# Expert output parts stacked on 128 partitions, gathered rows as half rows on 128 partitions, and the last output tile by weight rows

## The reference, cut to what matters

```python
def hier_moe(x, w_group, w_expert, w_gate, w_up, w_down):
    ...
    weight = g_w * e_w / jnp.sum(e_w, -1, keepdims=True)
    expert = (g_idx * M_PER_GROUP + e_idx).reshape(-1)
    token = jnp.repeat(jnp.arange(n_tok), M_TOPK)
    order = jnp.argsort(expert)
    tok_sorted = token[order]
    sizes = jnp.bincount(expert, length=M_EXPERTS).astype(jnp.int32)
    xs = xt[tok_sorted]
    hid = jax.nn.silu(lax.ragged_dot(xs, w_gate, sizes)) * lax.ragged_dot(xs, w_up, sizes)
    ys = lax.ragged_dot(hid, w_down, sizes) * weight.reshape(-1)[order][:, None].astype(x.dtype)
    return jax.ops.segment_sum(ys, tok_sorted, num_segments=n_tok).reshape(b, s, d)
```

## Time and profile before

| what | us |
|---|---|
| median of 3 runs | 2735.05 |
| range of the runs | 2734.01 to 2735.18 |
| time of the profiled execution | 2735.55 |
| its span, first to last instruction | 2733.7 |
| PE busy | 2618.6 (96%) |
| DVE busy | 1461.6 (53%) |
| ACT busy | 749.7 (27%) |

### The profile page before, as it was taken

One profiled execution on the slowest core, in us unless ns is written; L12 is line 12 of the kernel. 1 busy time (PEld: TensorE's weight loads), 2 busy tenths in 40 slices (PEclk: granted clock), 3 DMA queues, 4 the chain that ended last, 5 costly groups with the idle time before them and its releaser, 6 DMA issues. The chain is left out here.

```text
span 2733.7 us, 39425 instructions
## 1 busy us (share of the span) xinstructions
PE 2618.6 (96%) x15526; PEld 1859.7 (68%) x15526; DVE 1461.6 (53%) x2028; ACT 749.7 (27%) x1205; POOL 114.4 (4%) x238
## 2 busy tenths in 40 slices
PE   8997999999799979999999699999999999999999
PEld 7674555555476665555555577888888877888887
DVE  4755444444654554444444676656552666556632
ACT  3530000000145510000000343543332454433331
POOL 0000000000000000000000000000000010000000
PEclk9998999999899989999999899999999999999999
DMA  6249999999322089999997132223332312223331
GB/s 171 82 169 373 388 409 408 411 407 401 116 77 93 37 309 388 405 405 403 408 405 299 53 106 77 93 77 102 99 123 93 101 62 93 78 93 99 102 123 54
DMA packets 168109, 559.82 MB, mean 205 GB/s; under 512 B 17394, under 2 KB 100914, under 8 KB 118322
## 3 DMA queue, kind: packets, MB, share of 16 engines
q1 hardware_dynamic: 162546, 549.68, 53.4%
q0 software_dynamic: 5440, 8.40, 1.0%
HBM read 561.17 MB, written 6.29 MB: 208 GB/s over the span
## 5 line engine op out<-in xcount | busy, mean ns | idle before, releaser
L1401 DVE TENSOR_TENSOR resid<-resid,ps 128x1024 f32<-128x1024 f32 x252 | 306.8, 1218 | 237.7 <-PE ps L1321 237.7
L229 PE MATMUL ps<-l_h_hi,l_w_hi 128*128 128x512 f32 x896 | 352.9, 394 | 0.0
L230 PE MATMUL ps<-l_h_lo,l_w_hi 128*128 128x512 f32 x896 | 348.8, 389 | 0.0
L231 PE MATMUL ps<-l_h_hi,l_w_lo 128*128 128x512 f32 x896 | 348.7, 389 | 0.0
L1308 PE MATMUL ps<-first_weights,moe_xsT 128*64 128x256 f32 x2688 | 326.2, 384 | 0.0
L2885 DVE TENSOR_TENSOR l_w_lo<-l_raw,l_w_hi 128x2048 fp32r<-128x2048 f32 x76 | 174.0, 2292 | 270.6 <-ACT l_w_hi L2630 270.3
L1308 PEld LDWEIGHTS ps<-first_weights,moe_xsT 128*64 128x64 f32 x2688 | 191.5, 137 | 133.0 <-issue 67.4
L1373 ACT ACTIVATE moe_ys_hi<-ps 128x512 fp32r<-128x512 f32 x64 | 38.2, 597 | 687.3 <-PE ps L1347 687.3
L2630 ACT ACTIVATE l_w_hi<-l_raw 128x2048 fp32r<-128x2048 f32 x76 | 145.6, 1918 | 180.6 <-PE ps L231 161.1
L229 PEld LDWEIGHTS ps<-l_h_hi,l_w_hi 128*128 128x128 f32 x896 | 168.2, 188 | 37.6 <-issue 2.9
L230 PEld LDWEIGHTS ps<-l_h_lo,l_w_hi 128*128 128x128 f32 x896 | 168.3, 188 | 35.4 <-issue 1.4
(11 more groups left out here) (611 smaller groups left out, 4621.8 us busy)
## 6 DMA issues: line engine op xcount, KB each, us to landing
first_weights<-in_moe_w_up SPq DMA_DIRECT2D x84, 1024.0 KB, 11.5
first_weights<-in_moe_w_down SPq DMA_DIRECT2D x84, 1024.0 KB, 10.4
first_weights<-in_moe_w_gate SPq DMA_DIRECT2D x84, 1024.0 KB, 11.2
first_ring<-in_moe_w_up SPq DMA_DIRECT2D x44, 1024.0 KB, 11.7
first_ring<-in_moe_w_down SPq DMA_DIRECT2D x44, 1024.0 KB, 10.7
l_raw<-in_ffn_up SPq DMA_DIRECT2D x44, 1024.0 KB, 5.1
first_ring<-in_moe_w_gate SPq DMA_DIRECT2D x40, 1024.0 KB, 10.9
l_raw<-in_w_in SPq DMA_DIRECT2D x22, 1024.0 KB, 5.2
```

Of the source, the lines that this page charges most:

```text
L229: pe.matmul(out, stationary[0], moving[0], start=first, stop=False)
L230: pe.matmul(out, stationary[0], moving[1], start=False, stop=False)
L231: return pe.matmul(out, stationary[1], moving[0], start=False, stop=last)
L1401: dve.tensor_tensor(row, row, sums(t), ALU.add).then_inc(added, 1)
```

## The change

1. **Stacked parts.** One tile `ys` of 128 partitions x 2 x 512 takes the place of `ys_hi` and `ys_lo`. For column half 0 the high part stands on partitions 0-63 and the low part on 64-127, for half 1 the other way round. A combine is now two products of 128 rows. ACT makes the high part in two copies of 64 partitions, DVE the low part in two subtractions of 64 partitions; a subtraction writes the partitions that it doesn't read. Both count up one semaphore, `parts_made` (with `sel`, three to a block), on which the next combine waits.
2. **Half rows.** `xs` is 128 partitions x 512: slot s takes columns 0-511 of its row on partition s and columns 512-1023 on partition 64 + s. The gathers read 128 half rows of 2 KB instead of 64 rows of 4 KB, `r.take` is twice the row's number plus the half, and `lay` makes it for 128 partitions at once, after both halves of PE's list. The 8 transposes now alternate between partitions 0-63 (into bank 0) and 64-127 (into bank 1). The gate sums move to bank 1 and the up sums and turned hidden values to bank 3.
3. **Waits on PE.** The waits on `hid_kept` at a block's start and on `ys_low` ahead of the down product go; one on `silued` ahead of the turn of the rows comes.
4. **The last token tile of the output products** goes by weight rows: both column halves over the first four blocks of weight rows, then both over the last four. After the first four SP may start pieces of expert 0 (four of the six: up and down in the first layer, gate and up in the second), the other two after the last product. The third `keep_rows` stands ahead of that wait on SP.

The diff, cut to its core:

```diff
@@ Routing.lay @@
         dve.wait_ge(x.listed, 1)
-        dve.tensor_copy(x.near[0:SLOTS, :], k.ps[0:SLOTS, 3, 0:COLS]).then_inc(x.near_kept, 1)
-        dve.wait_ge(x.near_kept, 1)
-        dve.scalar_tensor_tensor(r.take[0:SLOTS, :], k.ps[0:SLOTS, 3, COLS:2 * COLS], float(NO_ROW), x.near[0:SLOTS, :], ALU.add, ALU.add).then_inc(x.done, 1)
+        link(dve.tensor_scalar(x.near[:, :], k.ps[:, 3, 0:COLS], float(NO_ROW), None, ALU.add))
+        link(dve.tensor_tensor(r.token, k.ps[:, 3, COLS:2 * COLS], x.near[:, :], ALU.add))
+        dve.tensor_scalar(r.take[:, :], r.token, 2.0, k.cst[:, C_HALF:C_HALF + 1], ALU.mult, ALU.add).then_inc(x.done, 1)
...
@@ window_layer, sync @@
             keep_rows(2)
+            sp.wait_ge(upper_used, 1)
+            weights.load(sp, layer, 0, 0, lambda c: None, range(2, 6))
             sp.wait_ge(am.out_made, 2 * NT)
-            weights.load(sp, layer, 0, 0, lambda c: None, range(6))
+            weights.load(sp, layer, 0, 0, lambda c: None, range(2))
...
@@ window_layer, out_part @@
-                half = q // 2
+                half, quarter = (q // 2, q % 2) if t + 1 < NT else (q % 2, q // 2)
...
@@ experts, tensor @@
             def turn_rows():
-                for j in range(ND):
-                    ins = pe.transpose(k.ps[:, TURN, j * SLOTS:(j + 1) * SLOTS], row_of_tile[:, j // 4, j % 4, :], k.cst[0:SLOTS, C_ID:C_ID + SLOTS])
+                for i in range(4):
+                    for c in range(2):
+                        rows_ = slice(64 * c, 64 * c + 64)
+                        ins = pe.transpose(turned[:, c, i * SLOTS:(i + 1) * SLOTS], row_of_tile[rows_, i, :], k.cst[rows_, C_ID + 64 * c:C_ID + 64 * c + 64])
...
                 if t == 0:
-                    wait_then_tick(pe, sel_made, b + 2, tick_pe)
-                    wait_then_tick(pe, ys_low, b + 2, tick_pe)
+                    wait_then_tick(pe, parts_made, 3 * b + 4, tick_pe)
...
-                for part in (ys_hi, ys_lo):
-                    for h in range(2):
-                        rows_ = slice(64 * h, 64 * h + 64)
-                        ins = pe.matmul(sums(t)[:, h, :], sel[rows_, t * P:(t + 1) * P], part[rows_, :], start=part is ys_hi, stop=part is ys_lo)
+                for h in range(2):
+                    ins = pe.matmul(sums(t)[:, h, :], sel[:, t * P:(t + 1) * P], ys[:, h, :], start=True, stop=True)
...
-                wait_then_tick(pe, ys_low, b + 1, tick_pe)
...
@@ experts, scalar @@
-                act.activation(ys_hi[:, :], k.ps[:, DOWN, :], ACT.Copy).then_inc(ys_kept, 1)
+                for h in range(2):
+                    rows_ = slice(64 * h, 64 * h + 64)
+                    act.activation(ys[rows_, h, :], k.ps[rows_, DOWN, :], ACT.Copy).then_inc(ys_kept, 1)
@@ experts, vector @@
-                dve.wait_ge(ys_kept, b + 1)
-                dve.tensor_tensor(ys_lo[:, :], k.ps[:, DOWN, :], ys_hi[:, :].bitcast(F32), ALU.subtract).then_inc(ys_low, 1)
+                for h in range(2):
+                    high, low = slice(64 * h, 64 * h + 64), slice(64 - 64 * h, P - 64 * h)
+                    dve.wait_ge(ys_kept, 2 * b + h + 1)
+                    dve.tensor_tensor(ys[low, h, :], k.ps[high, DOWN, :], ys[high, h, :].bitcast(F32), ALU.subtract).then_inc(parts_made, 1)
```

More of the change, by code:

```diff
@@ L426, in lay @@
         ins.then_inc(x.laid, 1)
[L427 to L430 removed]
+        dve.wait_ge(x.listed, 2)
         link(dve.tensor_copy(x.near[:, :], k.ps[:, 7, 0:COLS]))
@@ L762, in out_part @@
             def out_part(t, q):
-                half = q // 2
+                half, quarter = (q // 2, q % 2) if t + 1 < NT else (q % 2, q // 2)
                 if q == 0:
                     pe.wait_ge(o_lo, WIN_DONE[t])
-                if q % 2 == 0 and 0 < 2 * t + half < 5:
+                if quarter == 0 and 0 < 2 * t + half < 5:
                     pe.wait_ge(am.evacuated, 2 * t + half)
-                if (t, q) == (3, 2):
+                if (t, q) == (3, 1):
                     pe.wait_ge(am.evacuated, 5)
-                for j in range(4 * (q % 2), 4 * (q % 2) + 4):
+                for j in range(4 * quarter, 4 * quarter + 4):
                     if t == 0 and half == 0 and j % 2 == 0:
@@ L775, in out_part @@
                                        [y[:, j % 2, half * 512:(half + 1) * 512] for y in (hi, lo)], j == 0, j == ND - 1)
-                if q % 2:
+                if quarter:
                     ins.then_inc(am.out_made, 1)
+                elif (t, half) == (3, 1):
+                    ins.then_inc(upper_used, 1)
             pe.wait_ge(ident_in, 16)
@@ L1205, in experts @@
     silu, hid, hidT = st.sb("silu", [P, 256]), st.sb("hid", [P, 256]), st.sb("hidT", [P, 2, P])
-    take, slot = st.sb("take", [SLOTS, 1], I32), st.sb("slot", [P, 2, 1])
-    ys_hi, ys_lo, sel, iota = st.sb("ys_hi", [P, 512], F32R), rt.ys_lo, rt.sel, rt.iota
-    (take_set, slot_set, rows_turned, xsT_kept, silued, hid_kept, hid_turned, hidT_kept, ys_kept, ys_low, sel_made, combined, added, tick_sp, tick_pool, tick_pe, chain,
+    take, slot = st.sb("take", [P, 1], I32), st.sb("slot", [P, 2, 1])
+    ys, sel, iota = rt.ys, rt.sel, rt.iota
+    (take_set, slot_set, rows_turned, xsT_kept, silued, hid_kept, hid_turned, hidT_kept, ys_kept, parts_made, combined, added, tick_sp, tick_pool, tick_pe, chain,
      expert_set, grown, first_hi) = (st.sem(n) for n in (
-         "take_set", "slot_set", "rows_turned", "xsT_kept", "silued", "hid_kept", "hid_turned", "hidT_kept", "ys_kept", "ys_low", "sel_made", "combined", "added",
+         "take_set", "slot_set", "rows_turned", "xsT_kept", "silued", "hid_kept", "hid_turned", "hidT_kept", "ys_kept", "parts_made", "combined", "added",
          "tick_sp", "tick_pool", "tick_pe", "chain", "expert_set", "grown", "first_hi"))
     rows_in = r.rows_in
-    row_of_tile = xs[:, :].rearrange("s (c p j) -> s c j p", c=2, j=4)
+    row_of_tile = xs[:, :].rearrange("s (p j) -> s j p", j=4)
     hid_of_tile = hid[:, :].rearrange("s (p j) -> s j p", j=2)
@@ L1216, in experts @@
     count = dict(min_val=1, max_val=MAX_BLOCKS - EXPERTS + 1)
-    TURN, UP_BANK, DOWN, GATE = 0, 1, 2, 3
-    gate_out = lambda rows: k.ps[rows, GATE, 0:256]
+    TURN, GATE, DOWN, UP_BANK = 0, 1, 2, 3
+    gate_out = lambda rows: k.ps[rows, GATE, 256:512]
+    turned = k.ps[:, TURN:GATE + 1, 0:256]
     up_out = lambda rows: k.ps[rows, UP_BANK, 256:512]
@@ L1326, in body @@
                 wait_then_tick(pe, xsT_kept, b + 1, tick_pe)
-                wait_then_tick(pe, hid_kept, b + 1, tick_pe)
                 for c in range(4):
@@ L1334, in body @@
                 wait_then_tick(pe, rows_in, b * 16 + 32, tick_pe)
+                wait_then_tick(pe, silued, b + 1, tick_pe)
                 turn_rows()
-                wait_then_tick(pe, hid_kept, b + 2, tick_pe)
+                wait_then_tick(pe, hid_kept, b + 1, tick_pe)
                 for c in range(2):
@@ L1569, in _ @@
             keep_rows(2)
+            sp.wait_ge(upper_used, 1)
+            weights.load(sp, layer, 0, 0, lambda c: None, range(4))
             sp.wait_ge(am.out_made, 2 * NT)
-            weights.load(sp, layer, 0, 0, lambda c: None, range(6))
+            weights.load(sp, layer, 0, 0, lambda c: None, range(4, 6))
             keep_rows(3)
@@ L1689, in out_part @@
             def out_part(t, e):
-                half = e // 4
+                half, quarter = (e // 4, e % 4) if t + 1 < NT else ((e // 2) % 2, 2 * (e // 4) + e % 2)
                 if e == 0:
                     pe.wait_ge(o_lo, 4 * (t + 1))
-                if e % 4 == 0:
+                if quarter == 0:
                     if (t, half) == (0, 0):
@@ L1699, in out_part @@
                         pe.wait_ge(am.evacuated, 2 * t + half)
-                for j in range(2 * (e % 4), 2 * (e % 4) + 2):
+                for j in range(2 * quarter, 2 * quarter + 2):
                     if t == 0 and half == 0 and j % 2 == 0:
```

56 lines of the change are left out of this document (27 added, 29 removed).

## The result

| what | us |
|---|---|
| kernel before, median of 6 runs | 2734.57 (2733.82 to 2735.65) |
| changed kernel, median of 6 runs | 2746.11 (2741.74 to 2750.80) |
| ratio after / before | 1.0044, 95% interval 1.0032 to 1.0056 |
| span of the profiled execution, before and after | 2733.7 and 2744.8 |

What follows compares the result with a forecast made beforehand. PE was taken to bound the expert loops, with DVE already deciding each block's first combine. Terms 45.4 - 21.1 - 6.4 - 2.6 - 1.0 + 0.5 = +14.8 on 2735.05 gave 2749.9 us; 8-in-10 range 2733 to 2768.

Steps and rivals of the forecast that it cites:

- First combine: Ahead of each block's first combine, PE waits 0.71 us more for DVE's second subtraction: +45.4 us over 64 blocks.
- The end of the range with overlapping subtractions: At each block's first combine, if the two subtractions overlapped by about 0.08 us: 0.61 added, +39.0 us in all.
- Turn of the rows: Before the turn of the hidden values, paired transposes take 0.66 us instead of 1.17; 0.33 less a block, -21.1 us.
- The rival of unpaired turns: At the turn of the rows, transposes don't overlap in pairs, so the -21.1 goes: 2771 us; chance 0.09, much of it partial.
- One wait fewer: Ahead of each block's down product, the removed PE wait saves 0.10 us: -6.4 us (3.2 to 9.6).
- The combines: Each combine's two products of 128 rows take 0.65 us, 0.01 less than before: -2.6 us (-5.1 to +2.6).
- The faster rival: In every combine, weights load while the piece ahead streams, saving 0.11 us each: 2724 us; chance 0.13.
- Once per layer: At each expert stage's start, the first turn is 0.5 us shorter, twice: -1.0 us; a later list adds up to 0.5.
- The +0.5 for the later list: In the second layer's `lay`, `r.take` waits for both list halves and takes one step more: up to 0.5 us.
- Half-row gathers: In the expert loops, twice the requests for the same bytes cost nothing, with 6 us of cover before the next turn.
- Pieces sooner, last tile by weight rows: At the expert stages' starts and in the output products: no PE wait on expert 0's pieces, adds covered, so 0.
- Transfers: In the expert loops, the rival that transfers bind, hiding PE's stalls so that nothing changes: 2735 us; chance 0.05.

Runs made afterwards that it cites:

- stacked_only: The kernel before with the stacked parts alone; waits, turn and last tile as before: 2783.76 us, ratio 1.0179.
- unstacked: The changed kernel with the stacked parts alone undone (one high copy, one subtraction, four products a combine): 2699.39 us, ratio 0.9869 to the kernel before.
- short_second: The changed kernel with the second subtraction cut to 64 of 512 columns, part of the expert sum left out: 2717.73 us, ratio 0.9932 to the kernel before.
- unstacked_plain: The unstacked kernel with a third PE wait ahead of the down product, on `silued` at b + 1: 2709.73 us, ratio 0.9911 to the kernel before.
- stacked_later: The changed kernel with each block's first combine moved behind the second gate and up piece: 2675.43 us, ratio 0.9785 to the kernel before.
- unstacked_later: The unstacked kernel with each block's first combine moved behind the second gate and up piece: 2676.84 us, ratio 0.9793 to the kernel before.
- last_tile: The kernel before with only the last output tile by weight rows and the expert pieces asked for sooner: 2734.99 us, ratio 1.0003.
- stacked_grouped: The stacked_later kernel with the third combine also moved, beside the fourth behind the turn of the hidden values: 2649.97 us, ratio 0.9690 to the kernel before.
- unstacked_wait: The unstacked kernel with a third PE wait ahead of the down product, on `parts_made` at 2 b + 1: 2716.70 us, ratio 0.9933 to the kernel before.

## Why the prediction was right, step by step

- **First combine.** Right in mechanism and size: 0.708 a block against 0.71, the second subtraction held until the first has ended (0.04 apart in stacked_only, 1.41 for the pair in the changed kernel), PE released 0.39 behind it. The end of the range with overlapping subtractions (0.61) is out. unstacked and short_second show the cause from both sides: without the second subtraction 0.678 of the block go, with a short one 0.470. The rule of the Trainium skill that stood beside it (VectorE: DVE Perf Modes, "Two Vector instructions with no wait between them") agrees with that gap of 0.04. One reading beside it was loose: the copy of `near[64:]` in the earlier trace rows doesn't cross from one half of the partitions to the other, it reads and writes 64-127 behind instructions that start at partition 0. What it shares with the second subtraction is that it starts on another partition than the instruction ahead.
- **Turn of the rows.** 0.70 against 0.66 forecast for the turn, and 0.346 by the weight load against 0.33 for the step, since the hidden values decide: they end at 427.28, and PE takes up the next turn 0.12 later, as read off. The rival of unpaired turns is out.
- **One wait fewer.** The step that was mis-sized. My rows gave 0.05 or 0.15, and I took the middle, 0.10; the runs price the wait at 0.15 (unstacked_plain, and 0.419 against 0.266 in the kernels themselves), the upper of the two. That is 9.6 where I had 6.4, most of the blocks' whole error of 3.5; the turn gave 1.0 more than forecast and the combines 0.9 less. The lower value came from the first combine, which has another order of waits and other values to work out.
- **The combines.** 0.65 was forecast, 0.632 (first) and 0.665 (others) came; -1.7 in all against -2.6. Right that nothing is halved: stacked_later and unstacked_later, 1.4 us apart, show it without the wait in the way. The faster rival, 0.11 less from each combine, did not appear.
- **Once per layer.** The first turn gave a little more than the 0.5 forecast: from it to the first piece it is 2.34 and 2.56 before, 1.72 and 1.77 after. The +0.5 for the later list did not come: POOL's first gather is 0.6 later against the products around it in the second layer, but the stage's start now releases the turn, as in the first layer.
- **Half-row gathers.** Free in the loop: median landing 6.4 us against 7.0 in the first loop, POOL's issue 1.02 us. In one place they were not: at the first layer's second turn PE waited 1.34 for the rows, because its clock had been up and the 64 products before took 7.13 us instead of 8.81; the gather itself took 8.07 from issue to landing, against 7.47 before. My 6 us of cover were those of a later block; at a stage's start there is less.
- **Pieces sooner, last tile by weight rows.** Nothing, and last_tile shows it alone: 1.0003.
- **Transfers.** PE waited for no piece inside either loop, as the prediction read it. But SP's waits were a weak argument for that: issue to landing grew from 9.5 to 13.0 us in the first loop of the kernel before, so its blocks of 15.54 ran a little ahead of the transfers too. The rival was nearer than its 0.05 says, and stacked_grouped meets it.
- **What wasn't in the sum.** Each layer's end lost 1.63 and 0.96 instead of 0.71: the granted clock was 0.50 and 0.66 there, behind the longer idle time. I counted 64 first combines in the loops and took the last of them, which stands at the layer's end, for one like the others.

Together: 45.3 - 1.7 - 20.4 - 11.3 = +11.8 from the blocks, where the prediction had 15.3; the measured medians are 11.5 apart. That these agree so well is partly luck: in the profiled executions the layers' ends (+2.6) and the stages that the code hardly touches (-2.6) happened to cancel.

## What to carry to other kernels

An edit that makes one engine's work shorter and another's longer is worth what the waiting engine gains: first find, for each place, whom the bound engine waits for, then add on that engine alone. Here the same products in half the instructions cost 47 us because they put 0.71 on DVE's path to PE, and moving the consumer one piece later made the whole question void. Where two kinds of work alternate on PE, grouping them was worth some 0.2 us for each change saved. And a queue that waits for the bound engine doesn't prove that transfers have room: look at the time from issue to landing at the loop's start and at its end. If it grows, the engine is living on what was loaded ahead.

## What the runs showed of the hardware that I had not expected

- A wait that is long satisfied, with its increment, cost PE 0.148 us where it stands behind the wait that decides, and 0.243 with a value of 2 b + 1 or 3 b + 1, worked out from the loop's register; without one the down product starts 0.27 to 0.30 after DVE's copy.
- PE's granted clock fell to 0.50 to 0.76 behind 2.47 us of idle time at a layer's end in nine of ten such places in five kernels with stacked parts (stacked_later kept 1.00 in one), and stayed at 1.00 behind 1.76 in the kernel before and behind 2.00 in short_second; behind 1.75 it was 1.00 in some kernels (both ends of unstacked) and 0.64 to 0.78 in others (both ends of unstacked_wait and unstacked_later, one of unstacked_plain). With two products that nobody reads in between it was 0.95 and 1.00. How long the idle time is does not settle it alone.
- ACT's two copies of 64 partitions, one behind the other, took 1.21, twice the 0.60 of one on 128 partitions: half the partitions save nothing there either.
- Six weight pieces (6.3 MB) landed every 15.34 us in kernels whose blocks took 15.05, 14.61 and 13.9 us, and the time from issue to landing grew along the loop until, at some 28 us, PE waited.
